# A decoder step on one core: the sample rows' z/u/v projection in four column groups, the first x weights in two transfers, the dt columns two places up the queue

## What is computed

```
a    = rmsnorm(h) * norm_mix_g
proj = a @ w_in                      # columns: z 512 | xbc 1024 | dt 8 | u 512 | v 512
xbc  = silu(conv_b + causal conv of width 4 over [state_conv, xbc])
dt   = softplus(dt + dt_bias)
y    = chunked state space scan(x, dt, B, C, state_ssm) + d_skip * x
y    = grouped_rmsnorm(y * silu(z)) * ssd_norm_g
m    = rmsnorm(gelu(u) * chunk_mix(layernorm(gelu(v)))) * mlp_out_g
h    = h + [y, m] @ w_out
h    = h + moe(rmsnorm(h))           # top 4 of 32 experts, 1024 -> 2048 -> 1024
h    = h + (p @ w_ple_proj) * sigmoid(rmsnorm(h) @ w_ple_gate)
out  = rmsnorm(h) * norm_final_g     # and the new states
```

## Time and profile before

| | before |
|---|---|
| median of three runs | 1139.0 us |
| profiled execution, first to last instruction (its span) | 1135.4 us |
| TensorE matmuls busy | 1083.5 us, 95% |
| TensorE weight loads busy | 443.0 us |
| VectorE busy | 380.5 us |
| ScalarE busy | 162.2 us |
| read from HBM | 429.03 MB |
| mean granted TensorE clock | 0.998 |

### The profile page before, as it was taken

The page is one execution under the profiler, slowest core; times in us unless marked ns, Lnnn a source line. Parts: engine busy times, 40 slices in busy tenths (PEclk is TensorE's granted clock), DMA queues, the critical chain, the costliest instruction groups (busy, mean ns, idle before and its releaser), DMA issues.

```text
span 1135.4 us, 16392 instructions
## 1 busy us (share of the span) xinstructions
PE 1083.5 (95%) x6480; PEld 443.0 (39%) x6480; DVE 380.5 (34%) x967; ACT 162.2 (14%) x365; POOL 32.9 (3%) x79
## 2 busy tenths in 40 slices
PE   9999999999999999999998899999989898989897
PEld 6663454333333333333333343333333333333344
DVE  3866565132222323222221323131313131312165
ACT  3543132000000000000001010000000000000023
POOL 2300130000000000000000000000000000000000
PEclk9999999999999999999999999999999999999999
DMA  9833967999999999999999999999999999999951
GB/s 302 302 119 122 379 244 308 427 428 426 429 426 427 429 427 430 428 427 431 427 431 428 427 429 425 429 426 429 428 427 431 427 429 429 427 431 427 428 202 42
DMA packets 41748, 433.86 MB, mean 382 GB/s; under 512 B 6105, under 2 KB 7265, under 8 KB 17134
## 3 DMA queue, kind: packets, MB, share of 16 engines
q1 hardware_dynamic: 40080, 428.48, 90.2%
q0 software_dynamic: 1424, 4.47, 1.2%
q10 hardware_dynamic: 206, 0.40, 0.1%
HBM read 429.03 MB, written 4.30 MB: 382 GB/s over the span
## 4 chain that ended last, share of the span: by engine, by line
PE 65%; DMA 29%; DVE 3%; ACT 2%; issue 1%; SPq 0%; DVEq 0%; ACTq 0%
DMA ring<-in_w_up_dram 29%; PE bank L1056 27%; PE bank L1102 11%; PE bank L1040 6%; PE bank L624 5%; PE bank L746 3%; PE bank L1024 3%; PE bank L648 1%; PE bank L1086 1%; DVE arena L1609 1%; PE bank L1131 1%; PE bank L606 1%; PE bank L1021 1%; PE bank L1092 1%; PE bank L856 1%
## 5 line engine op out<-in xcount | busy, mean ns | idle before, releaser
L1056 PE MATMUL bank<-ring,aT 128*64 128x512 f32 x1536 | 346.6, 596 | 30.2 <-DMA ring<-in_w_up_dram 29.9
L1056 PEld LDWEIGHTS bank<-ring,aT 128*64 128x64 f32 x1536 | 105.9, 136 | 255.0 <-issue 197.6
L1102 PE MATMUL bank<-ring,arena 128*64 128x512 f32 x768 | 169.6, 594 | 0.2
L2031 DVE TENSOR_TENSOR h<-h,bank 128x512 f32<-128x512 f32 (+1 forms) x90 | 61.6, 684 | 174.3 <-PE bank L1040 172.1
L1056 PE MATMUL bank<-arena,aT 128*64 128x512 f32 x512 | 115.7, 596 | 3.5 <-DMA arena<-in_w_up_dram 3.5
L2048 DVE TENSOR_SCALAR arena<-bank 128x256 f32<-128x256 f32 x64 | 27.2, 424 | 237.8 <-PE bank L1056 236.5
L1416 ACT ACTIVATE arena<-arena 128x256 f32<-128x256 f32 x64 | 26.7, 417 | 549.6 <-DVE arena L2048 549.6
L2057 DVE COPY aT<-bank 64x512 f32<-64x512 f32 x32 | 22.2, 694 | 244.9 <-PE bank L1102 244.9
L1102 PEld LDWEIGHTS bank<-ring,arena 128*64 128x64 f32 x768 | 53.8, 137 | 100.9 <-issue 98.2
L1040 PE MATMUL bank<-aT,arena 128*32 128x512 f32 (+1 forms) x180 | 78.3, 622 | 0.0
L1056 PEld LDWEIGHTS bank<-arena,aT 128*64 128x64 f32 x512 | 35.3, 136 | 77.7 <-issue 69.8
(11 more groups left out here) (372 smaller groups left out, 764.9 us busy)
## 6 DMA issues: line engine op xcount, KB each, us to landing
ring<-in_w_up_dram SPq DMA_DIRECT2D x96, 2048.0 KB, 32.7
ring<-in_w_down_dram SPq DMA_DIRECT2D x48, 2048.0 KB, 33.8
arena<-in_w_up_dram SPq DMA_DIRECT2D x32, 2048.0 KB, 33.1
arena<-in_w_down_dram SPq DMA_DIRECT2D x16, 2048.0 KB, 33.9
ring<-in_w_in_dram SPq DMA_DIRECT2D x3, 2048.0 KB, 13.5
ring<-in_w_in_dram SPq DMA_DIRECT2D x4, 1024.0 KB, 11.4
ring<-in_w_out_dram SPq DMA_DIRECT2D x1, 4096.0 KB, 14.3
ring<-in_w_ple_gate_dram SPq DMA_DIRECT2D x2, 2048.0 KB, 13.5
```

The lines of the kernel that those rows point to most:

```text
L1056: mm = pe.matmul(bank[n][CAP * hf:CAP * hf + CAP, :], xT[:, odd, 2 * j + a, :], up_cols(x, j, a, hf, n), start=False, stop=(j == 3 and a = ...
L1102: mm = pe.matmul(bank[4][CAP * hf:CAP * hf + CAP, :], actT[:, b, t, :], tile_of(x, UP_TILES + t)[:, 1024 * b + 512 * hf:1024 * b + 512 * h ...
L2031: tt(part, part, bank[5 + j % 2][at:at + ROWS[c], :], ALU.add).then_inc(s_free[j % 2], 1)
```

## The change

`zuv2` now has four matmuls for each k, into all four groups of 32 partitions. Group g computes the columns 128g to 128g + 127 of z, u and v, 384 in all, which it reads as three runs. The scaling on VectorE covers 128 x 384; ScalarE's work on the result is cut into four pieces for z (32 x 128) and four for u and v together (32 x 256). The row scale is copied to a fourth group of partitions.

At the start the x weights come in five pieces (k = 0, k = 1, then two k each), and the dt columns are issued after the third of them, ahead of the last two. The gain vector is loaded as eight rows of 128 and turned with one transpose. One idle matmul stands behind each x tile in place of one behind each half, and the four behind the last are gone. The remaining parameter rows move up by one, to 32 in place of 33.

```diff
@@ plan_psum @@
-    jobs += [("zuv2", 3, 7)] + ...
+    jobs += [("zuv2", 8, 7)] + ...
@@ build @@
+        uvs = view(3840, 2, NCH, MLP)
-        prow = view(15872, 1024)
+        prow, grow = view(15872, 1024), view(16896, P)
+        w_zuv3 = ring[:, 8192:20480].rearrange("p (t k n) -> p t k n", t=3, k=KD)
+        XBC_PIECES = [slice(0, 1), slice(1, 2), slice(2, 4), slice(4, 6), slice(6, 8)]
@@ SP @@
-            for q in range(4):
-                sp.dma_start(w_xbc[:, 2 * q:2 * q + 2, :], w_in[:, 2 * q:2 * q + 2, SSD:o]).then_inc(xbc_in[q], 16)
-            with nc.allow_non_contiguous_dma(reason="eight dt columns"):
-                sp.dma_start(w_dt, w_in[:, :, o:o + HEADS]).then_inc(S["dt_in"], 16)
+            for q, ks in enumerate(XBC_PIECES):
+                sp.dma_start(w_xbc[:, ks, :], w_in[:, ks, SSD:o]).then_inc(xbc_in[q], 16)
+                if q == 2:
+                    with nc.allow_non_contiguous_dma(reason="eight dt columns"):
+                        sp.dma_start(w_dt, w_in[:, :, o:o + HEADS]).then_inc(S["dt_in"], 16)
@@ TensorE @@
-            for k in range(KD):
-                mm = pe.transpose(o[:, k:k + 1], prow[0:1, k * P:(k + 1) * P], ident[0:1, 0:1])
-            close_bank("gx", mm)
+            close_bank("gx", pe.transpose(o[:, 0:KD], grow[0:KD, :], ident[0:KD, 0:KD]))
...
                     transposed(("xT", c, hf), h, c, 4 * hf)
-                    keep_clock(1, 7, idle_rows)
-            keep_clock(4, 7, idle_rows)
+                keep_clock(1, 7, idle_rows)
...
-                        pe.wait_ge(xbc_in[k // 2], 16)
+                        pe.wait_ge(xbc_in[k if k < 2 else k // 2 + 1], 16)
...
-                pe.transpose(o[:, 33 * k:33 * k + 33], prow[0:33, k * P:(k + 1) * P], ident[0:33, 0:33])
+                pe.transpose(o[:, 32 * k:32 * k + 32], prow[0:32, k * P:(k + 1) * P], ident[0:32, 0:32])
...
-                for n in range(3):
-                    mm = pe.matmul(o[T_S * n:T_S * n + T_S, :], aT[:, k, TOK[2]], w_zuv[n][:, k, :],
+                for g in range(4):
+                    mm = pe.matmul(o[T_S * g:T_S * g + T_S, 0:3 * P], aT[:, k, TOK[2]], w_zuv3[:, :, k, P * g:P * g + P],
                                    start=(k == 0), stop=(k == KD - 1))
@@ ScalarE @@
-            act.dma_start(prow[0:1, :], I["norm_mix_g"]).then_inc(S["g_in"], 16)
+            act.dma_start(grow[0:KD, :], I["norm_mix_g"][0].rearrange("(k p) -> k p", p=P)).then_inc(S["g_in"], 16)
...
-            for n, (dst, f) in enumerate(((zs, ACT.Silu), (us, ACT.Gelu_apprx_tanh), (vs, ACT.Gelu_apprx_tanh))):
-                act.activation(dst[0:T_S, 2, :], o[T_S * n:T_S * n + T_S, :], f).then_inc(freed("zuv2"), 1)
+            for g in range(4):
+                act.activation(zs[0:T_S, 2, P * g:P * g + P], o[T_S * g:T_S * g + T_S, 0:P], ACT.Silu).then_inc(freed("zuv2"), 1)
+            for g in range(4):
+                act.activation(uvs[0:T_S, :, 2, P * g:P * g + P],
+                               o[T_S * g:T_S * g + T_S, P:3 * P].rearrange("p (t n) -> p t n", t=2),
+                               ACT.Gelu_apprx_tanh).then_inc(freed("zuv2"), 1)
@@ VectorE @@
-            for n in range(1, 3):
+            for n in range(1, 4):
                 n_rep = put(dve.tensor_copy(rs_x[T_S * n:T_S * n + T_S, 2:3], rs_x[0:T_S, 2:3]))
...
-            three = slice(0, 3 * T_S)
-            ts(o[three, :], o[three, :], rs_x[three, 2:3], None, ALU.mult).then_inc(S["zuv_ok"], 1)
+            ts(o[:, 0:3 * P], o[:, 0:3 * P], rs_x[:, 2:3], None, ALU.mult).then_inc(S["zuv_ok"], 1)
```

More of the change, by code:

```diff
@@ L62, in plan_psum @@
     jobs += [(("yd", 0), 1, 2), (("yd", 1), 1, 3), ("yo1", 1, 4), (("yd", 2), 1, 5)]
-    jobs += [("zuv2", 3, 7)] + [(("ns", 0, t), 4, (2, 3, 4, 5)) for t in range(4)] + [(("v", 0), 1, 6)]
+    jobs += [("zuv2", 8, 7)] + [(("ns", 0, t), 4, (2, 3, 4, 5)) for t in range(4)] + [(("v", 0), 1, 6)]
     jobs += [(("ns", 1, t), 4, (0, 1, 2, 3)) for t in range(4)] + [(("v", 1), 1, 7), ("hf", 1, 4)]
@@ L261, in build @@
             "gm_in pre_ok root_ok xact_ok xdtd_ok xt_full xt_ready y_full y_ok y_out ygs yn_ok yo_ok ysb_ok z_in")
-        xbc_in = [ctx.enter_context(nc.semaphore(f"xbc_in{q}")) for q in range(4)]
+        xbc_in = [ctx.enter_context(nc.semaphore(f"xbc_in{q}")) for q in range(5)]
         x_in = [ctx.enter_context(nc.semaphore(f"x_in{c}")) for c in range(NCH)]
@@ L672, in _ @@
             for k in range(KD):
-                pe.transpose(o[:, 33 * k:33 * k + 33], prow[0:33, k * P:(k + 1) * P], ident[0:33, 0:33])
+                pe.transpose(o[:, 32 * k:32 * k + 32], prow[0:32, k * P:(k + 1) * P], ident[0:32, 0:32])
             pe.wait_ge(S["pbr_in"], 16 * 3)
-            mm = pe.matmul(o[:, 264:264 + 3 * HEADS], ones[0:1, :], pbrow, start=True, stop=True)
+            mm = pe.matmul(o[:, 256:256 + 3 * HEADS], ones[0:1, :], pbrow, start=True, stop=True)
             close_bank("par", mm)
@@ L1182, in step @@
                 act.wait_ge(S["ach"], n_done[0])
-            act.dma_start(prow[0:1, :], I["norm_mix_g"]).then_inc(S["g_in"], 16)
[L1186 to L1192, removed]
+            act.dma_start(grow[0:KD, :], I["norm_mix_g"][0].rearrange("(k p) -> k p", p=P)).then_inc(S["g_in"], 16)
+            act.dma_start(prow[0:24, :], I["state_conv"][0].rearrange("b k n -> (b k) n")).then_inc(S["par_in"], 16)
+            act.dma_start(prow[24:28, :], I["conv_w"][0]).then_inc(S["par_in"], 16)
+            act.dma_start(prow[28:29, :], I["conv_b"]).then_inc(S["par_in"], 16)
+            act.dma_start(prow[29:30, 0:SSD], I["ssd_norm_g"]).then_inc(S["par_in"], 16)
+            act.dma_start(prow[29:30, SSD:D], I["mlp_out_g"]).then_inc(S["par_in"], 16)
+            act.dma_start(prow[30:31, :], I["norm_moe_g"]).then_inc(S["par_in"], 16)
+            act.dma_start(prow[31:32, :], I["norm_ple_g"]).then_inc(S["par_in"], 16)
             act.dma_start(pbrow[:, 0:HEADS], I["dt_bias"]).then_inc(S["pbr_in"], 16)
@@ L1215, in _ @@
             act.activation(xps[:, :, 0:3, :],
-                           o[:, 0:33 * KD].rearrange("p (k n) -> p k n", k=KD)[:, :, 1:25]
+                           o[:, 0:32 * KD].rearrange("p (k n) -> p k n", k=KD)[:, :, 0:24]
                            .rearrange("p k (b j) -> p k j b", b=B_S), ACT.Copy).then_inc(freed("par"), 1)
@@ L1580, in _ @@
                 ts(rdiag[r, c, 0:ROWS[c]], ident[r, 0:ROWS[c]], rs_x[r, c:c + 1], None, ALU.mult).then_inc(S["rdiag_ok"], 1)
-            for n in range(1, 3):
+            for n in range(1, 4):
                 n_rep = put(dve.tensor_copy(rs_x[T_S * n:T_S * n + T_S, 2:3], rs_x[0:T_S, 2:3]))
             o = filled(dve, "par")
-            dve.tensor_copy(pf[:, :, 0:8], o[:, 0:33 * KD].rearrange("p (k n) -> p k n", k=KD)[:, :, 25:33])\
+            dve.tensor_copy(pf[:, :, 0:8], o[:, 0:32 * KD].rearrange("p (k n) -> p k n", k=KD)[:, :, 24:32])\
                .then_inc(freed("par"), 1)
-            dve.tensor_copy(pb[:, :], o[:, 264:264 + 3 * HEADS]).then_inc(freed("par"), 1)
+            dve.tensor_copy(pb[:, :], o[:, 256:256 + 3 * HEADS]).then_inc(freed("par"), 1)
             dve.wait_ge(freed("par"), PS["par"][2] + 2)
```

## The result

| | before | after |
|---|---|---|
| median of 20 runs each, taken in turn | 1138.34 us | 1134.68 us |
| profiled execution: time | not given | 1134.26 us |
| its span | 1135.4 us | 1132.5 us |
| mean granted TensorE clock | 0.998 | 0.996 |

The ratio after to before is 0.9977, 95% interval 0.9969 to 0.9985: faster by 0.23%. The medians lie 3.7 us apart and the spans of the two profiled executions 2.9 us; forecast were 2.28.

What follows compares the result with a forecast made beforehand. The expert loop was taken as bound by the stream of expert weights, whose start TensorE sets. Savings of 1.71 (column groups) and 0.57 (start) made 2.28 us: span 1133.1, median 3.6 above, 1136.7 us; range 1135.9 to 1138.4.

Steps and rivals of the forecast that it cites:

- Four column groups: z/u/v projection of the sample rows: 16 steps of 384 columns, 5.29 us for 7.00, saving 1.71 us.
- the 5.3 us of cover: VectorE's normalised v is complete at 119.25, used at 124.56; ScalarE's extra pieces, up to 3.0 us, can't use that up.
- rival 5: A later wait takes part of the z/u/v saving of 1.71 us, ScalarE's pieces likeliest: 1137.8 us, chance 0.05.
- The start: First x projection: split weights and fewer idle matmuls let k = 0 run before k = 1 arrives, saving 0.57 us.
- rivals 1 and 2: First x weights: the split buys nothing, 1137.3 us, chance 0.14; or both halves come early, 1136.3 us, chance 0.08.
- the forecast's second wait, until 10.7: First x projection: TensorE does k = 0 from 9.8 us, then waits until 10.7 for k = 1.
- taken as equal: Eight parameter transposes with 32 rows for 33, and the copies that read them: no change in time.
- The dt columns and the idle matmuls: At the start: dt columns two places up, no gain, no loss; the idle matmuls cost hardly anything today.
- The median stands 3.6 us above that span: Last step of the sum: 3.6 us added to the predicted span of 1133.1 us to give a median of 1136.7.
- No gain: Gain vector's one transpose for eight, at the start: saves nothing, since the second x tile is waited for until 7.20 us.
- Rival 4: The clock falls near the first projection, which the idle matmuls may have prevented: 1138.5 or 1140.3 us, chance 0.06.
- the line at 1136.7: Border between faster and same, 0.2% or 2.28 us; faster was given 0.45, same 0.52, slower 0.03.

Runs made afterwards that it cites:

- idle_late: The changed kernel with two more idle matmuls in the 0.65 us wait at 164 us, ahead of expert 0; 1134.02 us, ratio 0.9965.
- before_look1: The kernel before, unchanged, profiled again; 1136.78 us, span 1135.0.
- before_look2: The kernel before, unchanged, profiled once more; 1138.88 us, span 1137.1.
- params_only: The kernel before with only the gain vector as 8 x 128 (one transpose) and 32 parameter rows; 1137.25 us, ratio 1.0000.
- params_back: The changed kernel with the gain vector as one row (eight transposes) and 33 parameter rows again; 1134.52 us, ratio 0.9975.
- before_again: The kernel before, unchanged, run and profiled a second time; 1138.84 us, ratio 0.9999.
- start_only: The changed kernel with three column groups again, so the new start alone; 1137.49 us, ratio 0.9986.
- idle_kept: The changed kernel with the start's seven idle matmuls put back; 1133.48 us, ratio 0.9967.
- before_twelve: The kernel before with twelve idle matmuls for eight ahead of the first transposes; 1137.44 us, ratio 0.9996.
- one_first: The changed kernel with the first x weights (k = 0 and 1) in one 1 MB transfer; 1136.01 us, ratio 0.9984.
- dt_back: The changed kernel with the dt columns back behind all x weights; 1134.71 us, ratio 0.9965.
- zuv_only: The kernel before with the four column groups alone; 1135.6 us, ratio 0.9974.
- idle_more: The changed kernel with the start's seven idle matmuls back and two more in the wait at 164 us; 1133.53 us, ratio 0.9951.
- best_twelve: idle_more with twelve idle matmuls for eight ahead of the first transposes; 1134.37 us, ratio 0.9966.
- dt_only: The kernel before with only the dt columns moved two places up; 1138.72 us, ratio 0.9998.

## Why the prediction was right, and where it was wrong

**Four column groups: right to a hundredth.** 5.29 us forecast, 5.30 measured, and 5.30 in every version that has them. The estimate that the forecast worked out beside the row from the speedups of a page gave 5.43 (the Trainium skill, "TensorE: Matmul & The Clock Gate", Part 3, measured speedup); the trace, at 5.30, disagrees with it. ScalarE's eight pieces and VectorE's scaling cost nothing: TensorE is busy for 93.67 of the 93.70 us from 59.6 to 153.3, so the 5.3 us of cover held and rival 5 did not come.

**The start: the mechanism right, the size too small.** Forecast 0.57; the first projection ends at 18.09 for 18.71, 0.62. The halves landed at 9.0 and 10.3 for 9.2 and 10.5, which refutes rivals 1 and 2. VectorE was done at 9.84 for 9.8, one weight load later, at 10.09, the projection began, and with k = 1 there at 10.3 the forecast's second wait, until 10.7, was hardly there. Where VectorE is done sooner it is there, as in `idle_late`:

```profile
9.49 0.72 PE L649 MATMUL bank<-aT,ring 128*128 128x288 f32 x2 [0.40 <-DMA ring<-in_w_in_dram]
10.41 7.54 PE L649 MATMUL bank<-aT,ring 128*128 128x288 f32 x30 [0.20 <-DMA ring<-in_w_in_dram]
```

Not priced was what comes behind it: 0.12 in the parameter transposes with their product, taken as equal, and about 0.28 between 31 and 36 us on VectorE, where two operations are shorter (2.64 us for 2.73 and 0.54 for 0.73). Together 0.99 at 59.63 for 60.62. A part of it is luck of the execution: other profiles of before with full speed in time have that operation at 60.25, 60.38 and 60.70.

**The dt columns and the idle matmuls:** no gain from either at the start, as priced.

**The step that failed** is the last of the sum: "The median stands 3.6 us above that span, so the forecast is 1136.7." It took 3.6 us for what lies around a span. Measured, a span and the time of the same execution are 1.76 us apart (1134.26 less 1132.5; 1136.78 less 1135.0 and 1138.88 less 1137.1 in `before_look1` and `before_look2`). The other 1.84 us was that the three runs shown, 1138.6 to 1139.23, were of the upper group and the profiled execution was of the lower. The forecast carried this over as if it were a constant, but after has no upper group. The gain vector's single transpose, with the rows that move with it, is the part that goes with that: of the nine full-clock runs of `params_only`, which has the one transpose of the gain vector, none is in the upper group, and the thirteen of after lie within 1 us of each other. That is the second failed step: the "No gain" of the gain vector's transpose. It holds for an execution like the profiled one; in those of the upper group, 52 of 86 at full clock, 2 us go with it. `params_back`, where the eight transposes are put back without a second level in the times, speaks against it, so what removes the group stays in part open. Put together: 1136.7 less 1.84, less 0.6 for the savings under-priced (2.9 for 2.28), plus 0.4 by which after's median, with seven fallen runs, lies above its profiled execution, is 1134.7.

**Rival 4** was the right worry, at the wrong place. It had the clock fall between 5 and 10 us for want of the idle matmuls. In no profile here did it fall there; what happens there is that full speed comes early or late, and it came as late as 10 us only in one profile of before and in `params_back`. The fall that does come is at 167 to 169 us in the three profiles that caught one (`before_again`, `start_only`, `idle_kept`). After has no such profile; its 7 runs with a fallen clock lie 2.8 to 4.8 us above the median of the others. The rule cited there, that transposes don't count as busy for the clock (the Trainium skill, the same page, Part 4), agrees with `params_back` and `before_look2`, where the speed stays low through the first twelve transposes and more. In `idle_late` full speed comes at 6.40 us with nothing but transposes running from 5.0 us on, but the eight idle matmuls end just ahead of them, so this neither bears the rule out nor contradicts it. The granted clock of after also reads half at 630 us, behind the first sixteen experts. This isn't the change's: 14 of the 18 profiles have it, among them four of the five of before, and the one that the forecast rested on is an exception. Expert 16's down product is 1.7 us later against expert 15's with it than without. By expert 31 the wait for the stream of weights has swallowed that, and it changes nothing in the end.

The chances were set about the line at 1136.7 with the forecast on it. Faster, at 0.45, is what came, and the kernel is faster like against like too, by 2.8 us. But the forecast stood on the line, and 1.84 of the 2.0 us by which the median lies below it are the wrong offset. That faster came so clearly is luck for the most part.

## What to carry to other kernels

Before a profile's span is set against a median, find out which of the groups of times the profiled execution belongs to; here the durations of a few equal matmuls at the start told it, where the granted clock of the stretch did not. Four column groups of a small product ran at the rate of the streamed columns here (0.33 us a step of 384 for 0.44 of 512), and the saving could be taken from a step of the same kind in the same trace. Where a stage of small products stands ahead of a long one, try idle matmuls in its waits and look at all the runs, not at the median: with two in a wait of 0.65 us none of 18 runs had a fallen clock, without them 35 of 91.

## What the runs showed that had not been expected

The first idle matmuls run at half speed while a stretch's granted clock says 1.00. By the first clock record full speed came at 4.0 to 5.3 us in eleven profiles, at 5.5 in `before_twelve`, between 5.7 and 6.6 in `idle_late`, `one_first`, `dt_back` and `idle_kept`, and at 10.0 in two, both of which had eight tiny transposes of one column behind the idle matmuls; seven other profiles with these transposes had it by 5.5. That the transposes are the cause is made likely by the runs of `params_only`, but not shown: that version also loads the gain vector in another way and has one parameter row fewer, and `params_back` has no upper group. How they would act is open.

One gain stays open. From expert 0 to expert 31 `zuv_only`, `start_only`, `idle_kept`, `idle_more`, `params_back` and `best_twelve` win 1.2 to 1.5 us against before, most of it between the down products of experts 22 and 23; after, `idle_late`, `one_first`, `dt_only`, `dt_back`, `params_only`, `before_twelve` and all the other profiles of before win 0.4 at most. So after, with both parts of the change, lacks a gain that each part alone has, and is at full clock 1.2 us behind the lower group of `zuv_only`, if in another set of runs. Timeline of TensorE, after, then `idle_more`:

```profile
827.26 3.65 PE L1057 MATMUL bank<-ring,aT 128*64 128x512 f32 x16 [0.70 <-DMA ring<-in_w_up_dram]
832.16 3.65 PE L1057 MATMUL bank<-ring,aT 128*64 128x512 f32 x16 [1.24 <-DMA ring<-in_w_up_dram]
837.05 3.65 PE L1057 MATMUL bank<-ring,aT 128*64 128x512 f32 x16 [1.24 <-DMA ring<-in_w_up_dram]
```

```profile
822.65 7.04 PE L1061 MATMUL bank<-ring,aT 128*64 128x512 f32 x32
830.79 3.65 PE L1061 MATMUL bank<-ring,aT 128*64 128x512 f32 x16 [1.09 <-DMA ring<-in_w_up_dram]
835.68 3.65 PE L1061 MATMUL bank<-ring,aT 128*64 128x512 f32 x16 [1.24 <-DMA ring<-in_w_up_dram]
```

In `idle_more` the first two of expert 23's tiles are both there, and the last comes 1.37 us earlier, while the DMA engines move 423 to 439 GB/s in both in every 5 us from 800 to 850. Why the tiles land so in one kernel and not in the other no run here tells.
